# Moving a triangular exponent from VectorE to ScalarE and repacking a ten-unit software pipeline

## The reference, cut to what matters

```python
gc = jnp.cumsum(blocks(g), axis=-1)
decay = jnp.exp(jnp.where(incl, gc[..., :, None] - gc[..., None, :], -jnp.inf))
kk = jnp.einsum('bhncd,bhnsd->bhncs', kc, kc)
a_mat = jnp.where(strict, bc[..., :, None] * kk * decay, 0.0) + jnp.eye(CHUNK)
sol = lax.linalg.triangular_solve(a_mat, rhs, left_side=True, lower=True, unit_diagonal=True)
qk = jnp.where(incl, jnp.einsum('bhncd,bhnsd->bhncs', qc, kc) * decay, 0.0)
```

## Time and profile before

| | us |
|---|---|
| median of 3 runs | 1655.38 (1654.91 to 1662.11) |
| the profiled execution, its own time | 1657.41 |
| its span, first to last instruction | 1655.6 |
| PE busy | 1581.2 (96%) |
| DVE busy | 1064.2 (64%) |
| ACT busy | 579.7 (35%) |
| POOL busy | 206.8 (12%) |

### The profile page before, as it was taken

The page is one execution under the profiler, slowest core; times in us unless marked ns, Lnnn a source line. Parts: engine busy times, 40 slices in busy tenths (PEclk is TensorE's granted clock), DMA queues, the critical chain, the costliest instruction groups (busy, mean ns, idle before and its releaser), DMA issues.

```text
span 1655.6 us, 27386 instructions
## 1 busy us (share of the span) xinstructions
PE 1581.2 (96%) x10579; PEld 1487.0 (90%) x10579; DVE 1064.2 (64%) x1965; ACT 579.7 (35%) x1106; POOL 206.8 (12%) x168
## 2 busy tenths in 40 slices
PE   5899999999999999998978999999999999999998
PEld 4899999999999999977867888989989999998886
DVE  5867666767364666545665788766887777763334
ACT  4522222221122533624444111245454444444223
POOL 0000000000000000120005666766100000000000
PEclk9999999999999999999998999999999999999999
DMA  9444444445244212220000000012212332312222
GB/s 278 125 145 129 140 145 146 131 136 165 83 133 141 90 51 72 57 64 27 26 1 7 1 1 1 1 32 59 66 56 65 90 88 76 98 47 84 77 77 89
DMA packets 183818, 136.62 MB, mean 83 GB/s; under 512 B 8192, under 2 KB 169269, under 8 KB 183605
## 3 DMA queue, kind: packets, MB, share of 16 engines
q1 hardware_dynamic: 161029, 112.91, 23.0%
q10 hardware_dynamic: 22704, 22.55, 4.5%
HBM read 132.03 MB, written 3.41 MB: 82 GB/s over the span
## 4 chain that ended last, share of the span: by engine, by line
PE 83%; DVE 10%; ACT 2%; SPq 2%; issue 2%; DMA 0%; POOL 0%; DVEq 0%; ACTq 0%; POOLq 0%
PE ps L2142 14%; PE ps L2144 13%; PE ps L2143 13%; PE ps L2302 5%; PE ps L2304 5%; PE ps L2303 5%; PE ps L2374 3%; PE ps L2786 3%; PE ps L2373 3%; PE ps L2372 3%; PE ps L2790 3%; SPq L503 2%; PE ps L2198 1%; PE ps L2568 1%; PE ps L2700 1%
## 5 line engine op out<-in xcount | busy, mean ns | idle before, releaser
L2142 PE MATMUL ps<-h_hi,w_lo 128*128 128x320 f32 x1152 | 366.0, 318 | 9.1 <-DVE h_lo L1310 4.0
L2144 PE MATMUL ps<-h_hi,w_hi 128*128 128x320 f32 x1152 | 357.4, 310 | 0.0
L2143 PE MATMUL ps<-h_lo,w_hi 128*128 128x320 f32 x1152 | 357.2, 310 | 0.0
L1263 DVE TENSOR_TENSOR w_lo<-w_raw,w_hi 128x1024 fp32r<-128x1024 f32 x120 | 148.9, 1243 | 259.9 <-ACT w_hi L674 259.2
L2142 PEld LDWEIGHTS ps<-h_hi,w_lo 128*128 128x128 f32 x1152 | 217.7, 189 | 15.0 <-DVE h_lo L1310 5.8
L2143 PEld LDWEIGHTS ps<-h_lo,w_hi 128*128 128x128 f32 x1152 | 217.8, 189 | 1.1 <-issue 0.7
L2144 PEld LDWEIGHTS ps<-h_hi,w_hi 128*128 128x128 f32 x1152 | 217.5, 189 | 0.0
L674 ACT CAST w_hi<-w_raw 128x1024 fp32r<-128x1024 f32 x120 | 125.6, 1048 | 211.0 <-PE ps L2144 110.3
L1397 DVE SCALAR_TENSOR_TENSOR ada_acc<-ada_ffn,cond,ada_acc 128x256 f32<-128x256 f32 x336 | 138.9, 478 | 1.1
L2142 PE MATMUL ps<-act_hi,w_lo 128*128 128x320 f32 (+1 forms) x352 | 109.6, 311 | 0.0
L2144 PE MATMUL ps<-act_hi,w_hi 128*128 128x320 f32 (+1 forms) x352 | 108.7, 309 | 0.0
(11 more groups left out here) (384 smaller groups left out, 3398.7 us busy)
## 6 DMA issues: line engine op xcount, KB each, us to landing
w_raw<-in_w_ffn_in SPq DMA_DIRECT2D x64, 512.0 KB, 4.0
w_raw<-in_w_ffn_out SPq DMA_DIRECT2D x44, 512.0 KB, 3.8
ada_ffn<-in_w_ada ACTq DMA_DIRECT2D x43, 512.0 KB, 3.9
w_raw<-in_w_in SPq DMA_DIRECT2D x28, 512.0 KB, 3.9
ada_ffn<-in_w_ffn_in SPq DMA_DIRECT2D x20, 512.0 KB, 4.1
ada_ffn<-in_w_ada SPq DMA_DIRECT2D x13, 512.0 KB, 4.6
ada_tile<-in_w_ada SPq DMA_DIRECT2D x10, 512.0 KB, 8.6
w_raw<-in_w_out SPq DMA_DIRECT2D x8, 512.0 KB, 3.4
```

Source lines behind the costliest of these rows:

```text
L1263: nc.vector.tensor_tensor(w_lo[at], w_raw[s][:], w_hi[at].bitcast(F32), ALU.subtract)\
L2142: nc.tensor.matmul(out, lo, xh, start=start, stop=False)
L2143: nc.tensor.matmul(out, hi, xl, start=False, stop=False)
L2144: return nc.tensor.matmul(out, hi, xh, start=False, stop=stop)
```

## The change

Two edits, tied by the semaphore counts.

First, stage 1 moves to ACT. Before: (sum - own sum) x mask on DVE. Now: eight `Relu` activations with scale -1 and the own sum as bias, which gives max(0, own sum - sum). Since the sums fall along the scan, this is the negated exponent inside the triangle and zero outside, so no mask is needed; the exponential then has scale -1. DVE's addition (L1910) waits for ACT in place of its own queue, and PE's products of stages 2 and 3, which overwrite the banks, wait for ACT too. DVE's count per unit falls from 23 to 21, ACT's rises from 3 to 5.

Second, the units begin at steps 0, 4, 8, 13, 26, 30, 34, 39, 52 and 56. A slot's next unit begins at the step after the last one's stage 25. The units whose ends matter end before step 60, 65, 78 and 82, and the marker work follows these: the first masks and products from 60 and 65, the next masks at 79 to 82, the three output pieces at 79 to 81. The weight remainder on DVE stays at `THREE_DONE + 9`, now step 74.

```diff
-PE_T, DVE_T, ACT_T, POOL_T = 24, 23, 3, 10
+PE_T, DVE_T, ACT_T, POOL_T = 24, 21, 5, 10
...
-MAKE_STAGES, MAKE_LAG = 26, 7
-TWO_DONE = 6 * MAKE_LAG + MAKE_STAGES
-THREE_DONE = TWO_DONE + MAKE_LAG
-FIRST_MASKS = [THREE_DONE + 9, THREE_DONE + 10, THREE_DONE + 12, THREE_DONE + 13]
+MAKE_STAGES = 26
+MAKE_START = [0, 4, 8, 13, 26, 30, 34, 39, 52, 56]
+TWO_DONE, THREE_DONE, ZERO_DONE, ONE_DONE = [MAKE_START[u] + MAKE_STAGES for u in (6, 7, 8, 9)]
+FIRST_MASKS = list(range(ZERO_DONE + 1, ZERO_DONE + 5))
...
-            for at in range((2 * NT - 1) * MAKE_LAG + MAKE_STAGES):
+            for at in range(ONE_DONE + 1):
...
-                    k = at - u * MAKE_LAG
+                    k = at - MAKE_START[u]
...
+                if k == 1:
+                    for d, x in ((0, x_w[c]), (1, t_cols[c])):
+                        q = 8 * d + 4 * g
+                        act.wait_ge(t_pe[c], r * PE_T + 1 + d)
+                        for h in range(4):
+                            ins = nc.scalar.activation(x[:, h, :], ps[:, 2 * c + d, h * P:(h + 1) * P], ACT.Relu,
+                                                       bias=gc[:, t, q + h:q + h + 1], scale=-1.0)
+                        ins.then_inc(t_act[c], 1)
                 if k == 3:
-                    act.wait_ge(t_dve[c], r * DVE_T + 3)
-                    nc.scalar.activation(x_w[c][:], x_w[c][:], ACT.Exp).then_inc(t_act[c], 1)
+                    act.wait_ge(t_dve[c], r * DVE_T + 1)
+                    nc.scalar.activation(x_w[c][:], x_w[c][:], ACT.Exp, scale=-1.0).then_inc(t_act[c], 1)
...
-                if k == 1:
-
-                    for d, x, m in ((0, x_w[c], "after"), (1, t_cols[c], "before")):
-                        q = 8 * d + 4 * g
-                        dve.wait_ge(t_pe[c], pe0 + 1 + d)
-                        for h in range(4):
-                            ins = nc.vector.scalar_tensor_tensor(x[:, h, :], ps[:, bank + d, h * P:(h + 1) * P],
-                                                                 gc[:, t, q + h:q + h + 1], const(m),
-                                                                 op0=ALU.subtract, op1=ALU.mult)
-                        ins.then_inc(t_dve[c], 1)
                 if k == 2:
-                    dve.wait_ge(t_dve[c], r * DVE_T + 2)
+                    dve.wait_ge(t_act[c], r * ACT_T + 4)
...
-                    if THREE_DONE + 11 <= c:
-                        n = c - THREE_DONE - 11
+                    if ONE_DONE - 3 <= c < ONE_DONE:
+                        n = c - ONE_DONE + 3
                         attention_part(n // 2, [n % 2])
...
                 if k == 2:
-                    pe.wait_ge(t_dve[c], dve0 + 1)
+                    pe.wait_ge(t_act[c], r * ACT_T + 3)
                     products(t, g, c, bank, 4, 0)
...
-                    pe.wait_ge(t_dve[c], dve0 + 2)
+                    pe.wait_ge(t_act[c], r * ACT_T + 4)
                     products(t, g, c, bank + 1, 0, 0)
```

More of the change, by code:

```diff
@@ L2088, in _ @@
                         mask_p(0, c - THREE_DONE)
-                    if c == THREE_DONE + 9:
+                    if c == ZERO_DONE + 1:
                         pool.wait_ge(t_dve[0], ROUNDS[0] * DVE_T)
@@ L2098, in _ @@
                 if k == 4:
-                    pool.wait_ge(t_act[c], r * ACT_T + 3)
+                    pool.wait_ge(t_act[c], r * ACT_T + 5)
                     pool.wait_ge(t_pool[c], pool0 + 1)
@@ L2102, in _ @@
                 if k == 6:
-                    pool.wait_ge(t_dve[c], dve0 + 4)
+                    pool.wait_ge(t_dve[c], dve0 + 2)
                     nc.gpsimd.tensor_tensor(tt, m_t[c][:], over4(const("level0")), ALU.mult).then_inc(t_pool[c], 1)
@@ L2112, in _ @@
                     else:
-                        pool.wait_ge(t_dve[c], dve0 + 8 + 3 * (n - 2))
+                        pool.wait_ge(t_dve[c], dve0 + 6 + 3 * (n - 2))
                     nc.gpsimd.tensor_tensor(tt_cols[c][:], tt, over4(const(f"sides{n}")), ALU.mult).then_inc(t_pool[c], 1)
@@ L2784, in _ @@
                 if n >= 1 and part == 0:
-                    pe.wait_ge(t_dve[c], dve0 + 6 + 3 * (n - 1))
+                    pe.wait_ge(t_dve[c], dve0 + 4 + 3 * (n - 1))
                     four(c, lambda out, h: nc.tensor.matmul(out, m_t[c][:, h, :], t_cols[c][:, h, :], start=True, stop=True))
                 if n >= 1 and part == 1:
-                    pe.wait_ge(t_dve[c], dve0 + 7 + 3 * (n - 1))
+                    pe.wait_ge(t_dve[c], dve0 + 5 + 3 * (n - 1))
                     pe.wait_ge(t_pool[c], pool0 + 4 + n)
@@ L2791, in _ @@
                 if n >= 1 and part == 2:
-                    pe.wait_ge(t_dve[c], dve0 + 8 + 3 * (n - 1))
+                    pe.wait_ge(t_dve[c], dve0 + 6 + 3 * (n - 1))
                     four(c, lambda out, h: nc.tensor.transpose(out, t_all[:, t, g, h * P:(h + 1) * P], ident[:]))
```

## The result

The changed kernel takes **1645.03 us** (median of 6 runs, 1641.20 to 1649.16), the kernel before 1655.50 on the same chip (6 runs). The ratio is 0.9925 with an interval of 0.991 to 0.994: 0.75% faster, more than the half per cent that the prediction gives as about what a measurement can tell from none. The forecast was 1643.2, range 1635 to 1652. In a later comparison the same kernel gave 1643.07 against 1657.35 (0.992, 0.9903 to 0.9937). The profiled execution took 1644.84 us with a span of 1643.0, against 1655.6 before.

The account below looks back on a forecast made before the run. The prediction took PE's waits in the make stage, largest behind DVE's queue, as the bound. Its terms summed to 212.7 us against 224.9, 12.2 less: 1645.2 for the profiled run, 1643.2 for the median, range 1635 to 1652.

Parts of the forecast that it names:

- opening, steps 0 to 12: Start of the make stage: 26.6 us against 39.8 for 21 steps before, with PE's clock falling to half again.
- a cycle: 26 steps for four units in the full pipeline: 74.7 us against 80.0, of which 2.9 are PE's waits.
- steps 60 to 64: Make stage's tail with three, then two units in flight: 11.9 us, by the same turns as the cycle.
- steps 65 to 71: Tail with two units and the first scan's products and states: 20.6 us, read from old steps 75 to 81.
- steps 72 to 77: Tail with two units alone: 10.6 us for a lone unit, 11.9 with the second unit's turns and weight remainder.
- What bounds the kernel: Make stage: PE has 17.95 us of work per 20.0 us unit; the rest is waits, the largest behind DVE's exponents.
- The exponents: Moving eight exponents per unit takes 2.07 us off DVE and adds 2.4 to ACT, which counts only in the opening.
- The starts: New unit starts keep four units in flight from step 13 to 59: 18.7 us a unit against 20.0.
- 1 (78 us a cycle): Rival: waits return elsewhere, at POOL and DVE; the gain is 6.3 us, 1649.1 us, no change; chance 0.20.
- 2 (71.8 a cycle, full clock): Rival: PE is the bound nearly everywhere and the opening takes 24.5 us; 1635.9 us; chance 0.10.
- 3, the clock: Rival: thin places lower PE's clock; 24 us of it cancel the gain, 45 us give 1665; chance 0.04.
- 4: Rival: ACT's queue makes the rectifiers late for PE in every unit; about 1655 us; chance 0.03.

Follow-up runs that it names:

- the later masks: Changed kernel with POOL's masks for the first scan at steps 61, 64, 65 and 65 instead of 61 to 64: 1644.64 us, stage 213.91.
- filled: Changed kernel plus 25 unread identity matmuls where PE stood idle in the opening: 1645.86 us (0.9928), repeated at 1642.47 us (0.9918).
- the doubled rectifiers: Changed kernel with eight more rectifiers per unit on ACT, into a tile nobody reads: 1649.57 us, 0.9945.
- even ones: Kernel before, exponents on DVE, with starts 6 or 7 steps apart (84 steps): 1651.28 us, one run.

## Why the prediction was right, point by point

| term | predicted | changed kernel | same kernel again |
|---|---|---|---|
| opening, steps 0 to 12 | 26.6 (24.5 to 30) | 29.99 | 26.21 |
| a cycle | 74.7 | 73.87 | 73.89 |
| middle, steps 13 to 59 | 134.5 | 133.36 | 133.37 |
| steps 60 to 64 | 11.9 | 12.85 | 12.85 |
| steps 65 to 71 | 20.6 | 19.72 | |
| steps 72 to 77 | 11.9 | 12.33 | |
| steps 78 to the scan | 7.2 | 7.20 | 39.26 for 65 to the scan (39.25 at the left) |
| stage | 212.7 | 215.45 | 211.69 |

- *What bounds the kernel.* Right: PE's waits, made by the order of DVE's queue. By the prediction's own count, 71.8 us a cycle for PE alone, the waits were 2.1 us instead of 2.9.
- *The exponents.* The rectifiers were priced 0.2 us too high and ended nearly when the prediction said: L1908 of unit 0 came 5.8 us behind the first product (877.87), predicted 6.1. That in a full pipeline they cost nothing is shown by doubling them.
- *The starts.* The number was right, but the text never asked what the starts do without the rectifiers. In the cycle they alone give nothing (81.71), the exponents alone 2.65, both 6.1. The turns were added up for both edits together, which is why the sum held.
- *Opening.* This is the term that was most off in the first profile, by 3.4 us; no other is off by more than 1.2. The step that failed is "then the products of units 1 and 2 in that step run at half speed": one low stretch with an end fixed by hand. In the first profile it began earlier, right behind the gap for ACT, and took both units' first products; in the second it ended sooner. A second miss, in both: "POOL's L2107 ends only 0.4 to 0.8 us before PE's transposes need it" was a little short in the cycle (the closest there is 0.05 us, 962.64 against 962.69, where an L2112 of 1.72 instead of 1.27 us stands in front), and failed for unit 1, where PE waited 1.58 us (900.81): ahead of its L2105 on POOL's queue stood unit 2's addition (896.54, 1.76 us) and unit 0's mask (898.27, 1.26 us). Steps 9 to 12 took 9.5 and 9.2 us, forecast 7.9. So the 26.21 of the second profile has luck in it: step 9 began 1.7 us early and the four steps behind it took 1.3 us too long.
- *Tail.* Steps 60 to 64 were 0.95 too low: the masks on POOL were charged nothing, with their cover named only for the next scan's. The wait of 1.35 us at 1047.76 is theirs, as the later masks show. Steps 65 to 71 gave 0.9 back: the 20.6 us were read from a stretch that ends with a wait of 0.78 us, which belongs to the step behind it, where one unit was left; now two are, and PE has no idle time there (1067.97). In steps 72 to 77 the weight remainder was priced at 0.88 us, read where POOL's mask ran beside it. It takes 2.31 us there and 1.22 now, and PE's idle time behind it is 0.28 (1074.03), so the second unit's turns have some 1.4 of the 12.33 us, where the sum had 0.4. The rows, two of the kernel before, then one of the changed kernel (its L1271 is L1263):

```profile
1086.28 1.16 PE L2790 MATMUL ps<-tt_cols,x_w 128*128 128x128 f32 x8 [0.78 <-DVE x_w L1921]
1089.52 2.31 DVE L1263 TENSOR_TENSOR w_lo<-w_raw,w_hi 128x1024 fp32r<-128x1024 f32 x1
```

```profile
1072.16 1.22 DVE L1271 TENSOR_TENSOR w_lo<-w_raw,w_hi 128x1024 fp32r<-128x1024 f32 x1
```

- *Sum against own time.* The stage gained 9.5 of the 12.2 forecast; 2.7 us that the profile before had ahead of the stage, by the scatter of its execution, made up for it in the span. So the profiled execution's 1644.84 meets the predicted 1645.2 with two errors that cancel, which is luck. When the kernel was profiled again, the stage's 211.69 was 1.0 from the predicted 212.7, with smaller errors of both signs; that execution took 1641.28, since it had 2.5 us less ahead of the stage than the one before.
- *Rivals.* 1 (78 us a cycle) fell at 73.87; it is close to what single edits give (75.95 to 81.71). 2 (71.8 a cycle, full clock) did not come even with the clock held up (filled: cycle 73.88, opening 25.9). 3, the clock, was the right place with the wrong size: some 7 or some 17 us of it, 3.8 us of time between executions, not 24 us of it. 4 fell with the doubled rectifiers.

## What to carry to other kernels

In a software pipeline on in-order queues, look at what stands in front of the awaited instruction, not only at an engine's load: DVE was busy for 80% of the cycle, and with crowded starts 2 us in the wrong place of its queue took back what two steps fewer a cycle gave with even ones (81.71 against 75.95, of which the clock has up to 3.3). Cross the edits with each other, every corner, before an edit is called worthless or the cause: one of the corners here refuted the story that three had told. Before calling a few microseconds in one profile a gain, take a second profile of the same kernel.

## What was not expected

**DVE and POOL take turns.** The addition L1908 (L1910 before), 128x512 with both inputs in SBUF, has lengths that the prediction did not explain: 0.69 us alone, 1.08 to 1.75 under a running POOL instruction. A timeline of both engines of the changed kernel:

```profile
958.46 1.27 POOL L2095 TENSOR_TENSOR tt_cols<-tt_cols,m_t 128x512 f32<-128x512 f32 x1
958.85 1.42 DVE L1908 TENSOR_TENSOR x_w<-x_w,t_cols 128x512 f32<-128x512 f32 x1
959.68 1.72 POOL L2112 TENSOR_TENSOR spare<-t_all,cst 128x512 f32<-128x512 f32 x1
...
961.53 1.16 PE L2784 MATMUL ps<-spare 128*128 128x128 f32 x8 [0.88 <-DVE spare L1928]
```

It ends 0.54 us after POOL's running instruction does (959.73 and 960.27). The same holds, within 0.02 us, for all 28 long ones in four profiles (before, rectifiers alone, and the changed kernel twice): with rectifiers alone it starts 0.73 us into POOL's instruction and takes 1.08, again to 0.54 behind its end; where POOL is idle it takes 0.69. The other way round, a POOL instruction that starts under it takes 1.31 to 1.77 instead of 1.27, and ends 1.12 to 1.15 us behind the addition's end. The weight remainder above is a third case: 2.31 us under POOL's mask, 1.22 alone. DVE's instructions with one input in PSUM (0.68 under a running POOL) show none of it. The Trainium skill, "SBUF — State Buffer", section "SBUF: two separate sides", says that VectorE with two SBUF inputs and GpSimd hold a shared port pair in turn, each for a whole instruction; the rows agree. The 0.7 us stand in front of L1928, for which PE waits 0.88. An order that keeps L1908 clear of POOL's work was not tried.

**The low clock has no fixed length.** The same kernel, with the same 2.85 us gap, had it for some 17 us in one execution and some 7 in another. What ends it is open.
